# Packed 64x64 blocks in the RWKV recurrence, and the first expert layer's bias added by VectorE

## The reference, cut to what matters

```
def step(S, inp):                                   # rwkv7_recurrence, scanned over 256 tokens
    r_t, w_t, k_t, v_t, a_t, b_t = inp
    Sa = einsum('bhvk,bhk->bhv', S, a_t)
    S = S * w_t + Sa[..., None] * b_t + v_t[..., None] * k_t
    return S, einsum('bhvk,bhk->bhv', S, r_t)
# then, per head: y = (y - mean) * rsqrt(var + LNX_EPS) * lnx_w + lnx_b, plus a bonus, times a gate g

def run_block(args):                                # expert layer
    tok, e = args
    h = x_pad[tok] @ w1[e] + b1[e]                  # b1: 2048 numbers per expert
    return clamped_swiglu(h) @ w2[e] + b2[e]        # even columns of h: glu, odd ones: lin
```

## Time and profile before

| | |
|---|---|
| median of 3 runs | 1401.48 us (1398.84 to 1402.33) |
| span of the profiled execution | 1400.3 us; no other time is recorded for this execution |
| TensorE (PE) busy | 1345.4 us, 96% of the span, 6334 MATMUL records |
| VectorE (DVE) / ScalarE (ACT) busy | 304.7 us / 199.0 us |
| DMA moved | 449.68 MB, mean 321 GB/s |
| granted TensorE clock, mean | 0.978 of full speed |

### The profile page before, as it was taken

One profiled execution on the slowest core, in us unless ns is written; L12 is line 12 of the kernel. 1 busy time (PEld: TensorE's weight loads), 2 busy tenths in 40 slices (PEclk: granted clock), 3 DMA queues, 4 the chain that ended last, 5 costly groups with the idle time before them and its releaser, 6 DMA issues.

```text
span 1400.3 us, 15803 instructions
## 1 busy us (share of the span) xinstructions
PE 1345.4 (96%) x6334; PEld 668.9 (48%) x6334; DVE 304.7 (22%) x477; ACT 199.0 (14%) x382; POOL 0.2 (0%) x4
## 2 busy tenths in 40 slices
PE   7999999999999999999999999999999999999995
PEld 6886799888845333233233333323333333332321
DVE  1256564241111101111011110111201112011112
ACT  1234421110011010011100111001111001110002
POOL 0000000000000000000000000000000000000000
PEclk9999999999997899999999999999999999999998
DMA  9343100159454899999999999999999999999993
GB/s 340 113 169 104 47 1 1 61 185 393 158 203 173 340 417 418 417 416 416 418 418 418 417 418 416 417 418 418 418 418 417 417 418 418 417 419 415 415 416 126
DMA packets 95164, 449.68 MB, mean 321 GB/s; under 512 B 8529, under 2 KB 20945, under 8 KB 62193
## 3 DMA queue, kind: packets, MB, share of 16 engines
q1 hardware_dynamic: 94828, 448.00, 80.0%
q10 hardware_dynamic: 292, 1.07, 0.2%
HBM read 447.99 MB, written 1.05 MB: 321 GB/s over the span
## 4 chain that ended last, share of the span: by engine, by line
PE 87%; DMA 5%; DVE 4%; issue 1%; SPq 1%; ACT 1%; PEldq 0%; DVEq 0%
PE ps L447 84%; DMA ring<-in_w_exp 3%; DMA upper<-in_w_exp 2%; PE ps L906 1%; SPq L412 1%; DVE upper L1414 1%; PE ps L665 1%; SPq L404 1%; DVE ring L1329 0%; PE ps L917 0%; DMA xrows<-in_x 0%; ACT ring L1106 0%; PE ps L463 0%; DVE ring L1419 0%; DVE ring L1420 0%
## 5 line engine op out<-in xcount | busy, mean ns | idle before, releaser
L447 PE MATMUL ps<-ring,upper 128*64 128x512 f32 (+4 forms) x2656 | 604.6, 579 | 10.6 <-PE ps L447 4.3
L447 PEld LDWEIGHTS ps<-ring,upper 128*64 128x64 f32 (+2 forms) x2656 | 207.8, 144 | 379.7 <-issue 362.5
L447 PE MATMUL ps<-upper 128*64 128x512 f32 (+6 forms) x1544 | 287.8, 459 | 7.1 <-PE ps L447 4.3
L447 PEld LDWEIGHTS ps<-upper 128*64 128x64 f32 (+3 forms) x1544 | 145.7, 166 | 144.8 <-issue 136.6
L447 PE MATMUL ps<-xT,ring 128*128 128x256 f32 x672 | 150.7, 382 | 0.0
L447 PEld LDWEIGHTS ps<-xT,ring 128*128 128x128 f32 x672 | 127.2, 191 | 19.3 <-issue 2.3
L1581 DVE TENSOR_TENSOR xrows<-xrows,ps 128x1024 f32<-128x1024 f32 x32 | 39.1, 1221 | 352.2 <-PE ps L447 352.2
L1565 DVE TENSOR_SCALAR upper<-ps 128x512 f32<-128x512 f32 x32 | 22.1, 691 | 420.7 <-PEq L886 420.7
L1204 ACT ACTIVATE upper<-upper 128x512 f32<-128x512 f32 x32 | 20.2, 630 | 536.9 <-DVE upper L1565 536.9
L447 PE MATMUL ps<-merged,cst 1*64 1x512 f32 x256 | 66.2, 633 | 0.0
L1210 ACT ACTIVATE factors<-ps 64x512 f32<-64x512 f32 x64 | 37.9, 591 | 199.5 <-PEq L901 198.8
(11 more groups left out here) (199 smaller groups left out, 521.8 us busy)
## 6 DMA issues: line engine op xcount, KB each, us to landing
ring<-in_w_exp SPq DMA_DIRECT2D x288, 1024.0 KB, 19.3
upper<-in_w_exp SPq DMA_DIRECT2D x96, 1024.0 KB, 19.2
ring<-in_w_gate SPq DMA_DIRECT2D x9, 1024.0 KB, 4.9
ring<-in_w_in SPq DMA_DIRECT2D x8, 896.0 KB, 11.6
ring<-in_w_in SPq DMA_DIRECT2D x8, 640.0 KB, 3.9
ring<-in_w_branch SPq DMA_DIRECT2D x5, 1024.0 KB, 5.1
ring<-in_w_mem_kv SPq DMA_DIRECT2D x4, 1024.0 KB, 4.9
ring<-in_w_out SPq DMA_DIRECT2D x4, 1024.0 KB, 13.2
```

The costliest lines, as they stand in the source:

```text
L447: return pe.matmul(o, l, r, start=start, stop=stop, skip_group_check=True)
```

## The change

**Constants and places.** The masks become 64 columns wide and stand for both halves of the partitions; a mask `eye` is new; the constants shrink from 2432 to 1920 columns. Gram matrices, inverse, t1, state and y are held in packed 64x64 blocks, at half the size. `ar` gets a third copy of r's block beside a's, so that either order of the two can be a stationary operand (`twin_sb`, one copy by ScalarE). The wide slots are used in another order and wait for other events.

```
-WIDE_AT = (8, 72, 80, 88, 96, 0, 16, 24, 32, 40)
+WIDE_AT = (88, 96, 8, 72, 80, 0, 16, 24, 32, 40)
                 elif s == NARROW:
-                    sp.wait_ge(t1_ps, 4 * (LEVELS - 1))
-                elif s == NARROW + 1:
-                    sp.wait_ge(yh_ps, 2)
+                    sp.wait_ge(pv_sb, 4)
+                elif s == NARROW + 2:
+                    sp.wait_ge(xx_ps, 2 * (LEVELS - 1))
+                elif s == NARROW + 3:
+                    sp.wait_ge(y_ps, NCH)
                 elif s == NARROW + 5:
-                    sp.wait_ge(y_rwkv_sb, 1)
+                    sp.wait_ge(y_rwkv_sb, TT)
```

```
+            corners = ((0, 0), (1, 1), (0, 1), (1, 0))
+            for n in range(4):
+                t, q = n // 2, n % 2
+                for i in range(2):
+                    for x, src in enumerate((bT, kT)):
+                        for a, c in corners:
+                            toks = slice(t * P + c * CH, t * P + (c + 1) * CH)
+                            last = mm(ps[rows64(c), 2 * n + a, (2 * i + x) * P:(2 * i + x + 1) * P],
+                                      src[rows64(a), 2 * q + i, toks], ar[rows64(a), (2 * q + i) * NCH + 2 * t + c, 1:3, :], i == 0 and x == 0)
+                last.then_inc(gram_ps, 1)
...
             for j in range(1, LEVELS):
+                for t in range(TT):
...
+                    for h in range(HP):
+                        for c, a in corners:
+                            last = mm(ps[rows64(a), 2 * t + c, h * 64:(h + 1) * 64], gram[rows64(c), 2 * t + h // 2, a, h % 2, 0, 0, :],
+                                      inv[rows64(c), t, h, a, :], h == 0)
                     last.then_inc(t1_ps, 1)
                     if j > 1:
+                        turn_inverse(t)
+                for t in range(TT):
+                    pe.wait_ge(t1_sb, 2 * (j - 1) + t + 1)
+                    pe.wait_ge(turned_sb, 2 * (j - 1) + t + 1)
+                    for h in range(HP):
+                        for a, c in corners:
+                            o = ps[rows64(c), 2 * t + a, h * 64:(h + 1) * 64]
+                            old, new = invT_a[rows64(a), t, h, c, :], t1s[rows64(a), t, c, h, :]
...
                     last.then_inc(xx_ps, 1)
```

```
+            for n in range(4):
+                dve.wait_ge(gram_ps, n + 1)
+                TTn(gram[:, n].rearrange("p a i x y t -> p (a i x) (y t)"), ps[:, 2 * n:2 * n + 2, :].rearrange("p a (k t) -> p (a k) t", k=4),
+                    const("causal").unsqueeze(1).to_broadcast([P, 8, P]), ALU.mult).then_inc(gram_sb, 1)
+                dve.wait_ge(gram_sb, n + 1)
+                base = invT[:, t, 2 * (n % 2):2 * (n % 2) + 2]
+                link(TTn(base, gram[:, n, :, :, 0, 0, :].rearrange("p a i t -> p i a t"),
+                         const("level0t").unsqueeze(1).unsqueeze(1).to_broadcast([P, 2, 2, CH]), ALU.mult))
+                link(TTn(base.rearrange("p h a s -> p (h a) s"), base.rearrange("p h a s -> p (h a) s"),
+                         const("eye").unsqueeze(1).to_broadcast([P, 4, CH]), ALU.add))
+                if n % 2:
+                    dve.transpose(flat(inv[:, t]), flat(invT[:, t])).then_inc(inv0_sb, 1)
```

```
             for ch in range(NCH):
                 if ch:
...
+                    for hp in range(HP):
+                        for a in range(2):
+                            last = mm(ps[:, bank + a, hp * 64:(hp + 1) * 64], ar[rows64(a), hp * NCH + ch, 1 - e:3 - e, :],
+                                      state[rows64(a), ch % 2, hp, :], hp == 0)
+                    last.then_inc(r_ps, 1)
+                if ch < NCH - 1:
+                    for h in range(HR):
+                        mm(ps[rows64(h % 2), 5, (h // 2) * 64:(h // 2 + 1) * 64], ktok[own, t, h * 64:(h + 1) * 64],
+                           vtok[own, t, h * 64:(h + 1) * 64], h < 2)
                 fill((ch, "a"))
...
                 for h in range(HR):
+                    last = mm(ps[own, 4, cols], invT[own, t, h // 2, a, :], rs_[own, cols] if ch else av[own, t, cols], h == 0)
...
+                    mm(ps[other, bank + a, (h // 2) * 64:(h // 2 + 1) * 64], gram[own, n, a, i, 1, 1, :], vtok[own, t, cols],
+                       ch == 0 and h < 2)
                 fill((ch, "b"))
                 pe.wait_ge(u_sb, ch + 1)
+                if ch < NCH - 1:
+                    for h in range(HR):
+                        last = mm(ps[rows64(h % 2), 5, (h // 2) * 64:(h // 2 + 1) * 64], btok[own, t, h * 64:(h + 1) * 64],
+                                  us[own, t, h * 64:(h + 1) * 64], False)
+                    last.then_inc(s_ps, 1)
+                for h in range(HR):
+                    last = mm(ps[other, bank + h % 2, (h // 2) * 64:(h // 2 + 1) * 64], gram[own, 2 * t + h // 4, h % 2, h // 2 % 2, 0, 1, :],
+                              us[own, t, h * 64:(h + 1) * 64], False)
+                last.then_inc(y_ps, 1)
                 fill((ch, "c"))
...
+            fill("norm0")
+            pe.wait_ge(y_sb, 3)
+            pe.wait_ge(ynorm_sb, 1)
+            turn_y(0)
+            fill("norm1")
+            pe.wait_ge(ynorm_sb, 2)
+            turn_y(1)
             fill("rest")
-            pe.wait_ge(y_rwkv_sb, 1)
+            pe.wait_ge(y_rwkv_sb, TT)
```

```
                     if c == 0 and bias:
+                        sp.wait_ge(b1_spread, g * GROUP + (r - 1))
...
-                        sp.dma_start(b1rows[at:at + 1, :], b_exp1[0, bass.ds(a * GROUP + r, 1), :]).then_inc(b1_full[r % 2], 16)
+                        for twice in range(2):
+                            at = 32 * twice
+                            sp.dma_start(b1rows[at:at + 65:64, r % 2, :],
+                                         b_exp1[0, bass.ds(a * GROUP + r, 1), :].rearrange("a (h f) -> (a h) f", h=2))\
+                              .then_inc(b1_full[r % 2], 16)

+            def spread_bias(E, N, parity, very_first=False):
+                dve.wait_ge(b1_full[parity], (N + 1) * 32)
+                if not very_first:
+                    dve.wait_ge(up_read, E)
+                dve.sem_inc(b1_here, 1)
+                dve.stream_shuffle(b1all, b1rows[:, parity, :], [0] * 32).then_inc(b1_spread, 1)

             def swiglu(E, very_first=False):
                 dve.wait_ge(up_ps, E + 1)
+                dve.wait_ge(b1_spread, E + 1)
...
-                TS(glu, ps[:, 0, :], LIMIT, None, ALU.min).then_inc(glu_sb, 1)
-                TS(lin, ps[:, 1, :], LIMIT, -LIMIT, ALU.min, ALU.max).then_inc(up_read, 1)
+                TTn(glu, ps[:, 0, :], b1all[:, 0:D:2], ALU.add).then_inc(glu_raw, 1)
+                TTn(lin, ps[:, 1, :], b1all[:, 1:D:2], ALU.add).then_inc(up_read, 1)
+                dve.wait_ge(glu_raw, E + 1)
+                TS(glu, glu, LIMIT, None, ALU.min).then_inc(glu_sb, 1)
                 dve.wait_ge(up_read, E + 1)
+                TS(lin, lin, LIMIT, -LIMIT, ALU.min, ALU.max).then_inc(lin_sb, 1)
```

More of the change, by code:

```diff
@@ L71 @@
 _at = 0
-for _n, _w in (("ident", P), ("heads", P), ("causal", 2 * P), ("level", LEVELS * P), ("level0t", P), ("before", P),
+for _n, _w in (("ident", P), ("heads", P), ("causal", P), ("level", LEVELS * CH), ("level0t", CH), ("eye", CH), ("before", P),
                ("ones", P), ("dist", 2 * P), ("iota", T), ("resets", T)):
@@ L111, in fill_points @@
 def fill_points():
-    points = [(ch, s) for ch in range(NCH) for s in "abc"] + ["mean", "var", "rest"]
+    points = [(ch, s) for ch in range(NCH) for s in "abc"] + ["norm0", "norm1", "rest"]
     counts = [1] * (3 * NCH) + [2, 3]
@@ L669, in _ @@
[L669 to L681 removed]
+            pe.wait_ge(pv_sb, 4)
@@ L684, in _ @@
+            pe.wait_ge(gram_sb, 2)
+            own_values(0, 0)
+            pe.wait_ge(gram_sb, 3)
+            pe.wait_ge(inv0_sb, 1)
+            turn_inverse(0)
+            pe.wait_ge(gram_sb, 4)
+            own_values(1, 6)
+            pe.wait_ge(inv0_sb, 2)
+            turn_inverse(1)
             for j in range(1, LEVELS):
-                late = {0: 3} if j == 1 else {0: 2, 1: 3}
-                for g in range(4):
-                    pe.wait_ge(inv_sb, 4 * (j - 1) + g + 1)
+                for t in range(TT):
@@ L758, in _ @@
             for ch in range(NCH):
-                t, c = ch // 2, ch % 2
-                rs = slice(64 * c, 64 * c + 64)
+                t, e = ch // 2, ch % 2
+                own, other = rows64(e), rows64(1 - e)
                 toks = slice(ch * CH, (ch + 1) * CH)
+                bank = 2 * (ch % 2)
                 if ch:
                     pe.wait_ge(s_sb, ch)
-                for hp in range(HP):
-                    last = mm(ps[rs, 0, hp * P:(hp + 1) * P], ar[:, hp, 0, toks], state[:, ch % 2, hp, :], hp == 0)
@@ L766, in _ @@
-                last.then_inc(r_ps, 1)
-                for hp in range(HP):
-                    mm(ps[:, 3, hp * P:(hp + 1) * P], ktok[rs, t, hp * P:(hp + 1) * P], vtok[rs, t, hp * P:(hp + 1) * P], hp == 0)
-                for hp in range(HP):
```

(46 more changed lines are left out.)

354 lines of the change are left out of this document (173 added, 181 removed).

## The result

The changed kernel takes 1349.74 us (median of 4 runs, 1348.86 to 1351.66), the kernel before 1401.33 beside it: ratio 0.962, 95% interval 0.958 to 0.966. Forecast were 1371 and a range of 1352 to 1386.

The account below looks back on a forecast made before the run. DMA was taken to bound the expert stage, TensorE what precedes it. Gains of 16.8 (A) + 9.6 (B) + 4.5 (C) + 0 (D) = 30.9 us took the span from 1400.3 to 1369.4; forecast 1371 us, range 1352 to 1386.

Parts of the forecast that it names:

- A: Gram matrices and inverse, up to the first chunk: small records at 40 ns, a gain of 16.8 us after the clock charge.
- A, levels: Inverse: 6.7 us for each of four levels and 5.3 for the first, 32.0 us in all.
- A, before level one: Gram matrices up to t1: VectorE later than TensorE, t1 starting at 176.7 instead of 180.3.
- A, the clock: Gram stage: TensorE idle about half of 12 us, so one clock drop, charged 3 us (between 0 and 8).
- B: The chunks in order: 336 records at 53 ns, 33.1 us of work becoming 23.5, a gain of 9.6 us.
- C: The bias at the start of the expert stage, at the first two experts: a gain of 4.5 us, between 1 and 7.
- D: The small DMAs of bias rows, one engine ending 8.2 us behind the mean: taken as 0, up to 9.4 either way.
- The frame: Expert stage paced by DMA: an earlier first `up` brings the end forward equally; shortening TensorE's later pairs brings nothing.
- the first: Rival for inverse and chunks: quarters overlap fully, 27 ns in the inverse and partly in the chunks, about 1356 us; chance 0.18.
- The second: Rival: low clock through the inverse, bias rows on one more loaded engine, or 53 ns records; about 1380 us; chance 0.26.
- the third: Rival for small records: calls in a quarter overlap nothing, 111 ns a record, slower than before at 1435 us; chance 0.04.
- the fourth: Rival between mixer and experts: SP's queue is held, loads start no earlier, only the bias gain is left, 1397 us; chance 0.04.

Follow-up runs that it names:

- the last run: The changed kernel with the small calls of the four chunks ordered by quarter, rotation in the inverse kept: 1356.32 us.
- the runs of the parts: Two runs: the kernel before with only the bias change, 1397.87 us; the changed kernel with the bias as before, 1351.78 us.
- the kernel with two quarters: The changed kernel with calls of Gram matrices, t1 and xx alternating between two quarters, then the other two: 1354.21 us.

## Why the prediction was wrong, and where it was right

**The step that failed** is the price in part A: "I take 40 ns, midway between 27 and 53", and below it the lower bound, "27 ns, if the two records of a call stay serial in their quarter at half the columns of the 53 ns case and all loads hide". They do stay serial in their quarter, at 58 ns. But the 53 ns case, at twice the columns, already was two streams side by side. The earlier trace rows held two twofold gains, 105 to 111 ns down to 52 by changing the row half and down to 53 by changing the column half. I used them as two witnesses of one limit, where they are two independent factors: 107 / 2 / 2 = 27 ns at N=128, and half of that at N=64. The measured 27 and 13.6 are just these. The lower bound was wrong, so the choice of 40 and the range were wrong with it. The rule held against packing, a floor of 27 ns a record, is not what this trace shows either.

- **A, levels.** At 13.6 ns the working's own terms make a level 1.75 + 0.9 + 0.7 = 3.35 us, and it took 3.93. By the rows of a level this is four groups of 32 loads, 3 x 0.56 + 0.59 = 2.27, two groups of turns, 0.84, and 0.82 between them. So 0.5 of the missing 0.6 is the last record of each group, which counts in full (0.137) and not as one distance, and 0.1 are the gaps. VectorE's answer, which the prediction called level with TensorE at short records, is not late: VectorE waits 0.52 us for TensorE before the second mask of a level. TensorE waits only 0.15, ahead of the second xx, for ScalarE's copy of the turned inverse:

```profile
181.61 0.69 DVE L1485 TENSOR_TENSOR ring<-ps,cst 128x512 f32<-128x512 f32 x1 [0.52 <-PE ps L460]
...
190.76 0.69 PE L460 MATMUL ps<-ring 64*64 64x64 f32 x32 [0.15 <-ACT ring L1159]
```

- **A, before level one.** t1 was forecast for 176.7 and came at 175.74; since the Gram matrices began 1.0 earlier too, the 12.5 us between were right. VectorE sets this time, as forecast: its four quarters end with the turn at 173.70 + 0.71, and TensorE's four transposes stand between that and t1. The turn of 128x512, taken as 0.7 without a row, took 0.71. So what A gained beyond the forecast, 32.1 for 16.8, lies behind this point: 19.6 us from t1 to the first chunk, where 32.0 were forecast and 3 more for the clock:

```profile
164.39 1.23 DVE L1472 TENSOR_TENSOR upper<-ps,cst 128x1024 f32<-128x1024 f32 x1 [5.46 <-PE ps L460]
...
173.70 0.71 DVE L1481 STREAM_TRANSPOSE ring<-ring 128x512 f32<-128x512 f32 x1
```

- **A, the clock.** One drop was forecast at 3 us, and one came, after TensorE had twice had no weight load for 1.76 us. The same groups at the low and the full level (1.78 and 1.01, 0.71 and 0.42, 1.80 and 1.15) make it about 1.7, an estimate:

```profile
172.00:178.00 6.00, 5.20 (x112) 4.61 (x116) 3.20 (x6) 1.78 (x3) 0.00 (x0) 0.50 0.01 3
178.00:196.00 18.00, 16.81 (x624) 13.99 (x617) 13.52 (x21) 4.78 (x8) 0.00 (x0) 0.98 0.01 4
```

- **B** gave 15.4 instead of 9.6, with the same fault. By the rows of each chunk its 336 records take 14.1 us (r 3 x 0.97, k times v 3 x 0.55, u with y 4 x 1.01, b times u with y 3 x 1.48, the last y 1.00), 42 ns each, and not 17.8 at 53, for k times v and u with y change the column half, at 27 and 28 ns. The expectation of the last run has u with y at 0.93 and the mean at 41; the trace has 1.01 and 42. The remaining 2.1 of the 5.8 that B gave more were not separated: changes of tile and waits that were fewer than counted are the likely place. The run with the chunks ordered by quarter shows that the price of these records is on the path.
- **C** was sized 4.5. The trace has 1.5 + 3.2, but the runs of the parts give 2.0 and 3.1, so 4.5 was somewhat too much; the rest may be the spread between single executions. The shuffle, bounded by 1.2 and 6.6 us, took 1.34 (near the lower), and the waits for the rows that VectorE has before it (92.6 us in all) cost nothing, since the pace is DMA's:

```profile
385.78 1.34 DVE L1639 STREAM_SHUFFLE upper<-merged 128x1024 f32<-128x1024 f32 x1
```
```profile
DVE upper L1639 <- DMA merged<-in_b_exp: 92.6, 23, 5.5
```

- **D** was rightly 0 as a difference (the lag goes from 8.2 to 9.1 us), but as a quantity it was the largest thing left: the rows cost the changed kernel 9 us. For the kernel before, whose lag of 8.2 us looks the same, no run asks it.
- **The frame** was right. All that TensorE gains before the expert stage arrives at the end: 50.1 us at the first `up`, 53.2 in the span, and 942.2 us between as forecast; the steady gain of TensorE's pairs is worth nothing (it is idle for 54.4 us in 600, 5.5 per pair, just as I named).

Of the rivals, the first (full overlap, 1356) was the nearest and had the right mechanism, but kept 27 ns. At a chance of 0.18 and with nothing below it, it left the range no room. Two slips of its working change nothing in this: a span of 1357 with the 1.2 us of the forecast is 1358, not 1356, and B at 27 ns sums to 14.8, not 14.4. The second (1380), the third (1435) and the fourth (1397) are refuted by the same rows; that the clock can hold through most of the inverse is shown by one of four executions of the kernel with two quarters, not by this one.

## What to carry to other kernels

When two rows each show a factor of two from two different causes, ask first whether the factors multiply, and put the product at the end of the range. Pack small blocks so that successive calls rotate over all quarters of the array: the order alone was worth 12 us in Gram matrices and inverse, and 7 in the chunks. And look at the end of a DMA-bound stage: a few engines that end late can mean that small transfers, by their shape, all go to the same engines. Here, loading such rows ahead of the stage, in four transfers of 32 partitions each, was worth 9 us.

## What the runs showed of the hardware that was not expected

- 64x64 float32 blocks (K=M=64, N=64) over four quarters: a record every 13.6 ns in the mean; in one quarter 58 ns; in blocks of eight records per quarter 41 ns; over two quarters, in blocks of sixteen, 23 ns.
- Weights of 64x128 with N=64 cost 52 ns when the row half changes at each call ((0.97 - 0.19) / 15, one such record lasting 0.19), just what N=128 costs in the earlier trace rows; so halving N alone, with 128 columns of weights, gained nothing.
- After the same idle in the Gram stage (twice 1.76 us without a weight load), TensorE's clock was at 0.98 over 178 to 196 in the changed kernel, and stayed at 0.50 there in one execution with two quarters at a time, though TensorE was busy for all 18.0 us of it. It cost that execution about 6 us. It is not the order's doing alone: the other three executions of the same kernel have a mean clock of 0.988, like the changed kernel, where this one has 0.981.
- A shuffle of 128x1024 on VectorE takes 1.34 us, a turn of 128x512 0.71 us, about as much as plain passes of these sizes (1.22 and 0.69).
